# Head norms on Trainium2: the means and the spreads of two neighbouring tiles, issued side by side on the two halves of the array

## The chip, the cores and the metric

The kernel runs on one NeuronCore of one Trainium2 chip. The metric is the time of one execution on the device in microseconds (us); lower is better. Engines are named as in the profile: PE (TensorE, matmul), PEld (its weight loads), DVE (VectorE), ACT (ScalarE), POOL (GpSimd), SP (SyncE, which issues the plain DMAs).

## The reference

Two transformer blocks, run one after the other on 512 tokens of width 1024, all in fp32. What matters here are the norms over a head, of which there are four kinds: queries and keys of the first block (16 heads of 64), queries and keys of the second block (8 heads of 64 each), and the two outputs of the second block's mixer (8 heads of 64, and 4 heads of 128).

```python
def first_block(...):
    h = rms_norm(x, norm1_g)
    q, k, v, bg, cg, xc = split(h @ w_in)
    q = rms_norm(q.reshape(b, nc, CHUNK, 16, 64), q_norm_g)
    k = rms_norm(k.reshape(b, nc, CHUNK, 16, 64), k_norm_g)
    ...                                   # attention, short convolution, gates, w_out, MLP

def second_block(...):
    h = rms_norm_2(x, g_norm1) * (1 + scale1) + shift1
    q_sb = rms_norm_2(to_heads(q_sb, 8), g_q_sb)
    k_sb = rms_norm_2(to_heads(k_sb, 8), g_k_sb)
    y_sb = rms_norm_2(stick_breaking(q_sb, k_sb, v_sb), g_out_sb)          # 8 heads of 64
    y_ml = rms_norm_2(mlstm(q_ml, k_ml, v_ml), g_out_ml) * sigmoid(o_ml)   # 4 heads of 128
    x = x + gate1 * (concat(y_sb, y_ml) @ w_out)
    x = x + gate2 * peer(h2, ...)         # 8 heads x 16 experts for each token, gathered from a table
```

## The kernel before

The 512 tokens go through in two halves of 256 (`hf` 0 and 1). Within a half the work is a fixed list of weight blocks (`SEQ`): each is 1 MB, 1024 rows by 256 columns, loaded by SP into a ring of four, and gives two output tiles `t` of 128 features by 256 tokens. A tile is eight fp32 matmuls, and each fp32 matmul stands in the records as two passes, so a tile is 16 passes and a block 32. A block's name says what it computes: Q1, K1, V1 (4 blocks each), CG, XC, BG, GC, CP, GA, AP, WO (4 each), UP and DN (16 each) for the first block; QKM (4), Q2, K2, V2, VM, OM (2 or 4), WO2 (4), PQ (8) for the second. The order of each engine's work is written out by hand (`half`), with semaphores between the engines.

**Head norms.** Activations lie with features on partitions, so one tile of 128 features holds two heads of 64, and the mean over a head is a sum over partitions. It is done by matmuls. For each of the eight tiles of a kind (`which` 0 to 3: Q1, K1, Q2 with K2, the mixer's output) ACT squares the tile into `scr` (L989, and L1202 for `which` 3), four buffers in turn. `head_mean` (L548 to 561) multiplies the squares by a narrow 128x64 matrix (`half_sel`, or `ml_sel` for heads of 128) that puts the tile's means into its own row of 64 rows of PSUM bank 5: tiles 0 to 3 accumulate in partitions 0 to 63, tiles 4 to 7 in partitions 64 to 127. ACT takes the square root (L1002), DVE the reciprocal (L1410, `hroot`). `head_spread` (L563 to 579) then spreads each row back over the 128 partitions of its tile by a matmul of 64 rows (`spread`, or one column of `ident`), and DVE multiplies the tile by it (`head_scale`, L1415), which counts `hn_done`. For `which` 0 to 2 two spreads share bank 4, side by side in its columns; for `which` 3 spread `i` goes to bank `i % 4`, and spreads 4 to 7 wait until the tile before in the same bank has been scaled.

**Where they stand on PE.** A mean is issued one tile late, so that ACT has had time to square: one after each tile of Q1 and K1 (L769 to 776), and of Q2 and K2. The spreads come two at a time, behind four of K1's and of V1's tiles, behind two of V2's, and around the 16 matmuls of the gates (`w_if`, L833), which accumulate in banks 6 and 7. For `which` 3 all eight means and then all eight spreads stand alone, between the mLSTM and WO2; ACT's squares 4 to 7 wait there for the means of the tiles whose buffer they take.

**Experts.** In half 1, and after it, the experts of half 0 are worked off: POOL gathers rows of 8 KB for 128 tokens (1 MB per slot) and DVE makes a dot product (L1310) and a scaled sum (L1337) of each. `tick` ties them to the weight blocks: behind most blocks of half 1 come two slots. What is left, some 310 of 512 slots, follows after half 1. In half 0 DVE instead sums up 24 modulation blocks (L1485, L1488) behind Q1, K1, V1, CG and XC.

Of the kernel before, what the change touches and what calls it, by code (L numbers as in the profile page):

```python
# [160 lines left out]
def build(nc, a, out):  # L161
    ctx = ExitStack()
    with ctx:
# [322 lines left out]
        def _(pe):  # L486
# [62 lines left out]
            def head_mean(hf, which, i):  # L549

                m = 32 * hf + 8 * which + i
                pe.wait_ge(sq_done, m + 1)
                if which == 3 and i >= 4:
                    sel = ml_sel[:, 3 - i % 4:67 - i % 4]
                else:
                    sel = half_sel[:, 6 - 2 * (i % 4):70 - 2 * (i % 4)]
                o = 64 * (i // 4)
                if i == 0 and which:
                    pe.wait_ge(rt_done, 4 * hf + which)
                pe.matmul(PS[o:o + 64, 5, 0:T], sel, scr[:, m % 4, :], start=i % 4 == 0, stop=i % 4 == 3, **LAX)\  # L560
                    .then_inc(ms_done, 1)

            def head_spread(hf, which, i):  # L563

                m = 32 * hf + 8 * which + i
                if i == 0:
                    pe.wait_ge(rr_done, 4 * hf + which + 1)
                b, c0 = (i % 4, 0) if which == 3 else (4, T * (i % 2))
                if which == 3 and i >= 4:
                    pe.wait_ge(hn_done, m - 3)  # L570
                if which < 3 and i >= 2 and i % 2 == 0:
                    pe.wait_ge(hn_done, m)
                o = 64 * (i // 4)
                if which == 3 and i >= 4:
                    sel = ident[o:o + 64, o + i % 4:o + i % 4 + 1].broadcast_to([64, P])
                else:
                    sel = spread[o:o + 64, 2 * (i % 4):2 * (i % 4) + 2, :].rearrange("p a b -> p (a b)")
                pe.matmul(PS[:, b, c0:c0 + T], sel, hroot[o:o + 64, :], start=True, stop=True, **LAX)\
                    .then_inc(hb_done, 1)
# [182 lines left out]
            def half(hf):  # L762
                for i in range(4):
                    for t in weights_block(NO[hf, Q1, i], h, fresh=4 * hf * KT if i == 0 else None):
                        if hf and 2 * i + t == 1:
                            pe.wait_ge(tok_copy, 10)
                        if 2 * i + t:
                            head_mean(hf, 0, 2 * i + t - 1)
                for which, kind in ((0, K1), (1, V1)):  # L769
                    for i in range(4):  # L770
                        for t in weights_block(NO[hf, kind, i], h, token_major=kind == V1):
                            j = 2 * i + t
                            if j == 0:
                                head_mean(hf, which, 7)
                            elif kind == K1:
                                head_mean(hf, 1, j - 1)
                            if 3 <= j < 7:
                                head_spread(hf, which, 2 * j - 6)
                                head_spread(hf, which, 2 * j - 5)
# [38 lines left out]
                for kind in (Q2, K2, V2):  # L818
                    for i in range(2):
                        for _ in weights_block(NO[hf, kind, i], h, token_major=kind == V2):  # L820
                            if 1 <= m <= 8:
                                head_mean(hf, 2, m - 1)
                            if m >= 10:
                                head_spread(hf, 2, 2 * m - 20)
                                head_spread(hf, 2, 2 * m - 19)
# [3 lines left out]
                head_spread(hf, 2, 4)  # L829
                head_spread(hf, 2, 5)  # L830
# [6 lines left out]
                head_spread(hf, 2, 6)  # L837
                head_spread(hf, 2, 7)
# [18 lines left out]
                for i in range(8):  # L857
                    head_mean(hf, 3, i)
                for i in range(8):
                    head_spread(hf, 3, i)  # L860
# [56 lines left out]
        def _(act):  # L917
# [165 lines left out]
            def half(hf):  # L1083
# [115 lines left out]
                for m in range(8):  # L1199
# [678 lines left out]
```

## Time and profile before

| what | value |
| --- | --- |
| device time, median of 3 runs | 2828.42 us |
| lowest and highest | 2819.37 and 2833.95 us |
| span of the profiled execution, first to last instruction | 2824.7 us |
| PE, DVE, ACT, POOL busy | 2248.1, 1806.8, 667.3, 766.6 us |
| mean granted clock of PE | 0.898 of full speed |
| half 0, first Q1 matmul to the first one of half 1 | 15.67 to 925.02 us |
| half 1, up to its last block's end | 925.02 to about 1992 us |
| experts that are left | about 1992 to 2824.7 us |

The page of the profile gives the span of the profiled execution and no device time of its own; the median of the runs is 3.7 us above that span. In a view of instructions in order of time the columns are the start, how long the group took, the engine, the line of the kernel, the operation with its tiles and shapes, how many were merged, and in brackets how long the engine had been idle before it and what ended that. Matmul records overlap, because a pass's end is drawn after the next one's start: what a matmul costs is read from start to start.

### The profile page before, as it was taken

The numbers are of one execution on the slowest core, as the hardware profiler recorded it, in microseconds if no ns is written. First come the engines' busy times: TensorE is split into PE (matmuls) and PEld (weight loads), VectorE is DVE, ScalarE is ACT, GpSimd is POOL, SyncE is SP. The second block draws the span as 40 slices with busy tenths as digits, with TensorE's granted clock in tenths as the row PEclk, the third lists the DMA queues.
The fourth block names the chain that finished last, engine by engine and source line by source line (L and its number), as shares of the span: only waits on it lengthen the run. The fifth ranks groups of instructions, "written<-read, shape, count | busy, mean of one in ns | idle before, by whom it ended". The sixth has DMA issues, their size and how long they took to land. (4 is left out here: it accounts for less than half of the span.)

```text
span 2824.7 us, 26350 instructions
## 1 busy us (share of the span) xinstructions
PE 2248.1 (80%) x9060; PEld 1659.6 (59%) x9060; DVE 1806.8 (64%) x3668; ACT 667.3 (24%) x1473; POOL 766.6 (27%) x544
## 2 busy tenths in 40 slices
PE   8999999999879998879999998978554555445554
PEld 6787788887668777657788776766211112111211
DVE  4663210012348678777777676759888888888886
ACT  2103212002612311553221126522211111111110
POOL 0000000000000244234433232212373555546551
PEclk9999999999889999999999998989787777777777
DMA  6774334433235699778999884546799999999996
GB/s 239 265 275 138 127 118 155 157 129 139 65 115 209 250 341 398 251 275 320 377 420 413 335 320 151 194 164 228 284 421 421 415 421 422 421 396 422 422 421 269
DMA packets 114661, 798.26 MB, mean 283 GB/s; under 512 B 13280, under 2 KB 16480, under 8 KB 19040
## 3 DMA queue, kind: packets, MB, share of 16 engines
q0 software_dynamic: 74880, 541.10, 47.2%
q1 hardware_dynamic: 39648, 255.47, 24.4%
q8 instruction: 73, 1.20, 0.2%
q14 instruction: 60, 0.49, 0.1%
HBM read 790.23 MB, written 6.29 MB: 282 GB/s over the span
## 5 line engine op out<-in xcount | busy, mean ns | idle before, releaser
L523 PE MATMUL PS<-reg,ring 128*128 128x256 f32 x6016 | 1361.7, 385 | 39.2 <-DVE reg L1405 10.6
L523 PEld LDWEIGHTS PS<-reg,ring 128*128 128x128 f32 x6016 | 1146.1, 193 | 227.0 <-issue 49.0
L473 POOL DMA_INDIRECT uv<-in_expert_uv,experts x322 | 502.3, 1560 | 1872.6 <-DVE experts L1292 879.4
L501 PE MATMUL PS<-uv,spare 128*128 128x512 f32 x276 | 188.4, 832 | 246.4 <-ACT spare L927 246.4
L1337 DVE SCALAR_TENSOR_TENSOR acc<-uv,coef,acc 128x1024 f32<-128x1024 f32 x249 | 319.9, 1285 | 9.0 <-DVE coef L1322 0.2
L1310 DVE CUSTOM_DVE_ANT_0 uv<-uv,h_tok 128x1024 f32<-128x1024 f32 x226 | 269.1, 1219 | 45.6 <-DMA uv<-in_expert_uv,experts 45.4
L501 PEld LDWEIGHTS PS<-uv,spare 128*128 128x128 f32 x276 | 69.8, 269 | 362.8 <-issue 362.8
L501 PE MATMUL PS<-reg,spare 128*128 128x512 f32 x228 | 154.0, 827 | 107.4 <-ACT spare L927 107.4
L934 ACT ACTIVATE acts<-dots 128x2 f32<-128x2 f32 (+1 forms) x192 | 39.1, 204 | 822.6 <-DVE dots L1310 778.1
L501 PEld LDWEIGHTS PS<-reg,spare 128*128 128x128 f32 x228 | 57.8, 267 | 203.0 <-issue 203.0
L473 POOL DMA_INDIRECT reg<-in_expert_uv,experts x114 | 147.8, 1297 | 77.2 <-PE PS L501 49.5
L1310 DVE CUSTOM_DVE_ANT_0 uv<-uv,reg 128x1024 f32<-128x1024 f32 x96 | 116.5, 1223 | 60.2 <-DMA uv<-in_expert_uv,experts 60.1
L1589 DVE TENSOR_TENSOR reg<-PS,reg 128x256 f32<-128x256 f32 x16 | 6.4, 420 | 219.2 <-PE PS L523 219.2
L501 PE MATMUL PS<-ring,spare 128*128 128x512 f32 x152 | 87.7, 716 | 59.6 <-ACT spare L927 59.6
L520 PE MATMUL PS<-ring,reg 128*128 128x256 f32 x512 | 119.3, 389 | 0.0
L473 POOL DMA_INDIRECT ring<-in_expert_uv,experts x76 | 107.1, 1409 | 38.4 <-issue 20.4
L1310 DVE CUSTOM_DVE_ANT_0 reg<-reg 128x1024 f32<-128x1024 f32 x96 | 112.8, 1221 | 3.8 <-DMA reg<-in_expert_uv,experts 3.8
L520 PEld LDWEIGHTS PS<-ring,reg 128*128 128x128 f32 x512 | 97.1, 194 | 19.0 <-issue 6.4
L934 ACT ACT_TABLE_LOAD x59 | 75.7, 1283 | 85.4 <-DVE dots L1310 46.6
L501 PEld LDWEIGHTS PS<-ring,spare 128*128 128x128 f32 x152 | 31.2, 219 | 109.2 <-issue 109.2
L1488 DVE SCALAR_TENSOR_TENSOR uv<-ring,silu_c,uv 128x256 f32<-128x256 f32 x168 | 81.4, 485 | 6.0
L1428 DVE SCALAR_TENSOR_TENSOR reg<-PS,toep 128x128 f32<-128x128 f32 (+1 forms) x64 | 30.9, 483 | 84.2 <-PE PS L603 84.2
(243 smaller groups left out, 2298.7 us busy)
## 6 DMA issues: line engine op xcount, KB each, us to landing
ring<-in_weights SPq DMA_DIRECT2D x228, 1024.0 KB, 5.4
uv<-in_expert_uv,experts POOLq DMA_INDIRECT x322, 12.9
reg<-in_x_t SPq DMA_DIRECT2D x2, 1024.0 KB, 6.2
kv_half<-reg SPq DMA_DIRECT2D x1, 2048.0 KB, 11.4
reg<-in_sub_t SPq DMA_DIRECT2D x2, 1024.0 KB, 4.7
toep<-in_rel_pad SPq DMA_DIRECT2D x16, 128.0 KB, 4.1
x_tokens<-reg SPq DMA_DIRECT2D x2, 1024.0 KB, 9.4
reg<-kv_half SPq DMA_DIRECT2D x1, 2048.0 KB, 16.2
```

The lines of the kernel that those rows point to most:

```text
L473: gp.indirect_dma_start(UV[r], None, a["expert_uv_2"], bass.IndirectOffsetOnAxis(ap=experts[:, e % 256:e % 256 + 1], axis=0))\
L501: mm = pe.matmul(PS[:, 6 + j, :], diag[:, n % 4, :], UV[BUF[s]][:, D + 512 * j:D + 512 * j + 512], start=begins, stop=ends, **LAX)
L520: mm = pe.matmul(out_tile(n, t), mv[:, t * P:(t + 1) * P], w, start=first and k == 0, stop=last and k == KT - 1)
L523: mm = pe.matmul(out_tile(n, t), w[:, t * P:(t + 1) * P], mv, start=first and k == 0, stop=last and k == KT - 1)
L934: act.activation(acts[:, s0 % 16:s0 % 16 + s1 - s0], dots[:, s0 % 16:s0 % 16 + s1 - s0], ACT.Gelu)\
L1310: dve.tensor_tensor_reduce(out=u, in0=u, in1=H2[s // 256][:, s // NSLOT % 2, :], scale=1.0, scalar=0.0, op0=ALU.mult, op1=ALU.add, accum_o ...
L1337: dve.scalar_tensor_tensor(acc[:, :], v, c, acc[:, :], ALU.mult, ALU.add).then_inc(acc_done, 1)
L1428: dve.scalar_tensor_tensor(PROB[:, i % 4, 0:w], PS[:, i % 3, 0:w], HD1 ** -0.5, toep[:, hd % 2, w - 1::-1], ALU.mult, ALU.add).then_inc(s_ ...
L1488: dve.scalar_tensor_tensor(ac, ring[:, n % NRING, k, :], silu_c[:, k:k + 1], ac, ALU.mult, ALU.add)\
L1589: dve.tensor_tensor(x[:, k, :], out_tile(n, t), x[:, k, :], ALU.add).then_inc(evac_sem(n, t), 1)
```

## The change

`head_means` issues the means of an even and an odd tile one right behind the other: the even tile's go to partitions 0 to 63 of bank 5 (columns 0 to 63 of the array), the odd tile's to partitions 64 to 127 (columns 64 to 127). It stands behind every second tile. `head_spreads` issues the spreads of such a pair in the same way: the even tile's row comes from rows 0 to 63 of the array, the odd one's from rows 64 to 127, and they write different banks (4 and 6; for `which` 3 `j` and `4 + j`, so none waits for a scaled tile). The gates' matmuls move from banks 6 and 7 to bank 7 alone. For `which` 3 the pairs are tile `j` of the stick-breaking output with tile `j` of the mLSTM output, and ACT writes its eight squares to eight buffers (`scr` and `spare`), so that none waits for a mean. The number of matmuls, squares and scales stays the same.

```diff
+        def spread_at(which, j, odd):
+            if which == 3:
+                return 4 * odd + j, 0
+            return 4 + 2 * odd, 0
+        def mixed_square(j, odd):
+            return (spare if odd else scr)[:, j, :]
...
-            def head_mean(hf, which, i):
...
+            def head_means(hf, which, j):
+                at = 32 * hf + 8 * which + 2 * j
+                if j == 0 and which:
+                    pe.wait_ge(rt_done, 4 * hf + which)
+                pe.wait_ge(sq_done, at + 2)
+                for odd in range(2):
+                    if which == 3 and odd:
+                        sel = ml_sel[:, 3 - j:67 - j]
+                    else:
+                        sel = half_sel[:, 6 - 2 * j:70 - 2 * j]
+                    src = mixed_square(j, odd) if which == 3 else scr[:, 2 * (j % 2) + odd, :]
+                    pe.matmul(PS[64 * odd:64 * odd + 64, 5, 0:T], sel, src, start=j == 0, stop=j == 3, **LAX)\
+                        .then_inc(ms_done, 1)
...
-            def head_spread(hf, which, i):
...
+            def head_spreads(hf, which, j):
+                if j == 0:
+                    pe.wait_ge(rr_done, 4 * hf + which + 1)
+                if which < 3 and j:
+                    pe.wait_ge(hn_done, 32 * hf + 8 * which + 2 * j)
+                for odd in range(2):
+                    o, (b, c0) = 64 * odd, spread_at(which, j, odd)
+                    if which == 3 and odd:
+                        sel = ident[o:o + 64, o + j:o + j + 1].broadcast_to([64, P])
+                    else:
+                        sel = spread[o:o + 64, 2 * j:2 * j + 2, :].rearrange("p a b -> p (a b)")
+                    pe.matmul(PS[:, b, c0:c0 + T], sel, hroot[o:o + 64, :], start=True, stop=True, **LAX)\
+                        .then_inc(hb_done, 1)
...
-                        if 2 * i + t:
-                            head_mean(hf, 0, 2 * i + t - 1)
+                        if i and t == 0:
+                            head_means(hf, 0, i - 1)
...
-                                head_mean(hf, which, 7)
-                            elif kind == K1:
-                                head_mean(hf, 1, j - 1)
+                                head_means(hf, which, 3)
+                            elif kind == K1 and t == 0:
+                                head_means(hf, 1, i - 1)
                             if 3 <= j < 7:
-                                head_spread(hf, which, 2 * j - 6)
-                                head_spread(hf, which, 2 * j - 5)
+                                head_spreads(hf, which, j - 3)
...
-                            if 1 <= m <= 8:
-                                head_mean(hf, 2, m - 1)
+                            if m in (2, 4, 6, 8):
+                                head_means(hf, 2, m // 2 - 1)
...
-                        mm = pe.matmul(PS[32 * g:32 * g + NML, 6 + g, 0:T], w_if[:, k, g * NML:(g + 1) * NML], H[:, k, :],
+                        mm = pe.matmul(PS[32 * g:32 * g + NML, 7, 0:T], w_if[:, k, g * NML:(g + 1) * NML], H[:, k, :],
...
-                for m in range(8):
-                    if m >= 4:
-                        act.wait_ge(ms_done, 32 * hf + 24 + m - 3)
-                    act.activation(scr[:, m % 4, :], mixed(m), ACT.Square).then_inc(sq_done, 1)
+                for j in range(4):
+                    for odd in range(2):
+                        act.activation(mixed_square(j, odd), mixed(j + 4 * odd), ACT.Square).then_inc(sq_done, 1)
...
-                for m in range(8):
-                    head_scale(hf, 3, m, mixed(m), col("g_out_sb", m))
-                    if m >= 4:
-                        dve.wait_ge(hn_done, 32 * hf + 25 + m)
-                        dve.tensor_tensor(mixed(m), mixed(m), OMT[:, m - 4, :], ALU.mult).then_inc(mixed_gain, 1)
+                for j in range(4):
+                    head_scale(hf, 3, j, 0, mixed(j), col("g_out_sb", j))
+                    head_scale(hf, 3, j, 1, mixed(j + 4), col("g_out_ml", j))
+                    dve.wait_ge(hn_done, 32 * hf + 26 + 2 * j)
+                    dve.tensor_tensor(mixed(j + 4), mixed(j + 4), OMT[:, j, :], ALU.mult).then_inc(mixed_gain, 1)
```

How the instructions stand on PE is shown at three places, before and after apart; the changed kernel's lines are numbered some nine higher, and `x8` of L523 (after: L532) is one tile. First PE in half 0, the last tiles of K1 and the first of V1 (L520, after L529), with K1's means (L560, after L570) and Q1's spreads (L578, after L585). Before:

```order
L523 MATMUL PS<-reg,ring 128x256 x8
L560 MATMUL PS<-scr,half_sel 64x256
L578 MATMUL PS<-hroot,spread 128x256 x2
L523 MATMUL PS<-reg,ring 128x256 x8
L560 MATMUL PS<-scr,half_sel 64x256
L578 MATMUL PS<-hroot,spread 128x256 x2
L523 MATMUL PS<-reg,ring 128x256 x8
L560 MATMUL PS<-scr,half_sel 64x256
L520 MATMUL PS<-ring,reg 128x256 x8
L560 MATMUL PS<-scr,half_sel 64x256
```

Now:

```order
L532 MATMUL PS<-reg,ring 128x256 x8
L585 MATMUL PS<-hroot,spread 128x256 x2
L532 MATMUL PS<-reg,ring 128x256 x8
L570 MATMUL PS<-scr,half_sel 64x256 x2
L585 MATMUL PS<-hroot,spread 128x256 x2
L532 MATMUL PS<-reg,ring 128x256 x8
L529 MATMUL PS<-ring,reg 128x256 x8
L570 MATMUL PS<-scr,half_sel 64x256 x2
```

Every second mean has moved behind the next tile, beside its neighbour; the spreads stand where they stood.

Second PE in half 0 from V2's last tile to the stick-breaking's first logits (L670, after L677), with the gates' matmuls (L833, after L837). Before:

```order
L520 MATMUL PS<-ring,reg 128x256 x8
L578 MATMUL PS<-hroot,spread 128x256 x4
L833 MATMUL PS<-reg,w_if 4x256 x16
L578 MATMUL PS<-hroot,spread 128x256 x2
L670 MATMUL PS<-reg 128x256
```

Now:

```order
L529 MATMUL PS<-ring,reg 128x256 x8
L585 MATMUL PS<-hroot,spread 128x256 x4
L837 MATMUL PS<-reg,w_if 4x256 x16
L585 MATMUL PS<-hroot,spread 128x256 x2
L677 MATMUL PS<-reg 128x256
```

Nothing has moved here; only rows of the array and banks differ.

Third ACT in half 0, the squares of the mixer's output (L1202, after L1204) and the square root behind them (L1002, after L1005). Before:

```order
L1202 ACTIVATE scr<-reg 128x256 x8
L1002 ACTIVATE hroot<-PS,epsc 128x256
```

Now:

```order
L1204 ACTIVATE scr<-reg 128x256
L1204 ACTIVATE spare<-reg 128x256
L1204 ACTIVATE scr<-reg 128x256
L1204 ACTIVATE spare<-reg 128x256
L1204 ACTIVATE scr<-reg 128x256
L1204 ACTIVATE spare<-reg 128x256
L1204 ACTIVATE scr<-reg 128x256
L1204 ACTIVATE spare<-reg 128x256
L1005 ACTIVATE hroot<-PS,epsc 128x256
```

The squares alternate between the two kinds of output and between two tensors.

## Rows read from the trace of the kernel before

**Rows 1.** The page's part on busy time, by engine: us, share, instructions.

```profile
PE 2248.1 (80%) x9060; PEld 1659.6 (59%) x9060; DVE 1806.8 (64%) x3668; ACT 667.3 (24%) x1473; POOL 766.6 (27%) x544
```

**Rows 2.** Stretches: length; PE, PEld, DVE, ACT, POOL busy; clock, DMA share, GB/s.

```profile
957.00:996.00 39.00, 39.00 (x165) 28.11 (x163) 24.66 (x38) 9.47 (x25) 15.22 (x9) 1.00 0.85 331
...
1659.00:1684.00 25.00, 25.00 (x108) 18.84 (x109) 13.26 (x19) 5.69 (x16) 9.79 (x6) 1.00 0.94 362
...
1992.00:2824.00 832.00, 418.84 (x680) 159.29 (x679) 703.92 (x1251) 133.26 (x336) 419.35 (x318) 0.76 0.97 401
```

**Rows 3.** PE in order of time: Q1 of half 0, and a stream without norms.

```profile
23.32 3.72 PE L523 MATMUL PS<-reg,ring 128*128 128x256 f32 x16
26.97 0.65 PE L560 MATMUL PS<-scr,half_sel 128*64 128x256 f32 x2
27.55 3.72 PE L523 MATMUL PS<-reg,ring 128*128 128x256 f32 x16
...
189.72 22.61 PE L523 MATMUL PS<-reg,ring 128*128 128x256 f32 x104
```

**Rows 4.** PE in order of time, K1 of half 0.

```profile
65.01 0.65 PE L560 MATMUL PS<-scr,half_sel 128*64 128x256 f32 x2
65.59 1.13 PE L578 MATMUL PS<-hroot,spread 64*128 64x256 f32 x4
66.64 3.72 PE L523 MATMUL PS<-reg,ring 128*128 128x256 f32 x16
```

**Rows 5.** PE in order of time: the gates, and the mixer norm's means, half 0.

```profile
705.38 3.62 PE L833 MATMUL PS<-reg,w_if 128*4 128x256 f32 x32
...
797.08 0.63 PE L560 MATMUL PS<-scr,half_sel 128*64 128x256 f32 x1
797.14 0.64 PE L560 MATMUL PS<-scr,ml_sel 128*64 128x256 f32 x1
797.51 0.63 PE L560 MATMUL PS<-scr,half_sel 128*64 128x256 f32 x1
```

**Rows 6.** PE in order of time: attention scores of two heads, half 1.

```profile
1135.81 0.70 PE L606 MATMUL PS<-reg 64*128 64x256 f32 x4
1136.35 0.59 PE L603 MATMUL PS<-reg 64*128 64x256 f32 x4
```

**Rows 7.** ACT in order of time, the mixer's norm of half 0.

```profile
794.41 1.33 ACT L1202 ACTIVATE scr<-reg 128x256 f32<-128x256 f32 x4 [1.22 <-DVE reg L1763]
...
799.79 0.47 ACT L1002 ACTIVATE hroot<-PS,epsc 128x256 f32<-128x256 f32 x1 [0.77 <-PE PS L560]
```

**Rows 8.** DVE in order of time, the mixer's norm of half 0.

```profile
803.07 0.48 DVE L1415 SCALAR_TENSOR_TENSOR reg<-reg,par,PS 128x256 f32<-128x256 f32 x1 [1.02 <-PE PS L578]
...
805.63 0.87 DVE L1415 SCALAR_TENSOR_TENSOR reg<-reg,par,PS 128x256 f32<-128x256 f32 x2 [0.37 <-PE PS L578]
...
806.87 0.47 DVE L1415 SCALAR_TENSOR_TENSOR reg<-reg,par,PS 128x256 f32<-128x256 f32 x1
807.38 0.42 DVE L1769 TENSOR_TENSOR reg<-reg 128x256 f32<-128x256 f32 x1
807.72 0.47 DVE L1415 SCALAR_TENSOR_TENSOR reg<-reg,par,PS 128x256 f32<-128x256 f32 x1
...
809.08 0.42 DVE L1769 TENSOR_TENSOR reg<-reg 128x256 f32<-128x256 f32 x1
```

**Rows 9.** PE in order of time, V1 and Q2 of half 1.

```profile
1012.59 1.13 PE L578 MATMUL PS<-hroot,spread 64*128 64x256 f32 x4 [1.73 <-DVE hroot L1410]
1013.65 5.41 PE L520 MATMUL PS<-ring,reg 128*128 128x256 f32 x16
...
1648.78 0.99 PE L560 MATMUL PS<-scr,half_sel 128*64 128x256 f32 x2 [5.11 <-ACT scr L989]
1649.71 5.01 PE L523 MATMUL PS<-reg,ring 128*128 128x256 f32 x16
```

**Rows 10.** Waits of DVE in half 1: who for whom, us, times, longest.

```profile
DVE reg L1523 <- DMA x_tokens<-reg: 11.9, 1, 11.9
```

More of the change, by code:

```diff
@@ L547, in rms @@
                         .then_inc(rms_mm, 1)
-            def head_mean(hf, which, i):
[L551 to L558, printed above, removed]
-                    pe.wait_ge(rt_done, 4 * hf + which)
-                pe.matmul(PS[o:o + 64, 5, 0:T], sel, scr[:, m % 4, :], start=i % 4 == 0, stop=i % 4 == 3, **LAX)\
-                    .then_inc(ms_done, 1)
@@ L764, in half @@
                     for t in weights_block(NO[hf, Q1, i], h, fresh=4 * hf * KT if i == 0 else None):
[L765 removed]
+                        if hf and 2 * i + t == 2:
                             pe.wait_ge(tok_copy, 10)
[L767 to L768 removed]
+                        if i and t == 0:
+                            head_means(hf, 0, i - 1)
                 for which, kind in ((0, K1), (1, V1)):
@@ L856, in half @@
                 mlstm(hf)
[L857 to L860, printed above, removed]
+                for j in range(4):
+                    head_means(hf, 3, j)
+                for j in range(4):
+                    head_spreads(hf, 3, j)
                 pe.wait_ge(hn_done, 32 * hf + 32)
@@ L1198, in half @@
                 act.wait_ge(ml_y, NML * (hf + 1))
-                for m in range(8):
-                    if m >= 4:
-                        act.wait_ge(ms_done, 32 * hf + 24 + m - 3)
-                    act.activation(scr[:, m % 4, :], mixed(m), ACT.Square).then_inc(sq_done, 1)
+                for j in range(4):
+                    for odd in range(2):
+                        act.activation(mixed_square(j, odd), mixed(j + 4 * odd), ACT.Square).then_inc(sq_done, 1)
                 head_root(hf, 3)
@@ L1410, in head_inverse, with head_scale @@
                 dve.reciprocal(hroot[:, :], hroot[:, :]).then_inc(rr_done, 1)
-            def head_scale(hf, which, i, tile, gain):
-                b, c0 = (i % 4, 0) if which == 3 else (4, T * (i % 2))
-                dve.wait_ge(hb_done, 32 * hf + 8 * which + (i if which == 3 else i | 1) + 1)
+            def head_scale(hf, which, j, odd, tile, gain):
+                b, c0 = spread_at(which, j, odd)
+                dve.wait_ge(hb_done, 32 * hf + 8 * which + 2 * j + 1 + (odd if which == 3 else 1))
                 dve.scalar_tensor_tensor(tile, tile, gain, PS[:, b, c0:c0 + T],
@@ L1513, in half @@
                             if 3 <= j < 7:
-                                head_scale(hf, which, 2 * j - 6, tiles[:, 2 * j - 6, :], col(gain))
-                                head_scale(hf, which, 2 * j - 5, tiles[:, 2 * j - 5, :], col(gain))
+                                head_scale(hf, which, j - 3, 0, tiles[:, 2 * j - 6, :], col(gain))
+                                head_scale(hf, which, j - 3, 1, tiles[:, 2 * j - 5, :], col(gain))
                         tick(hf, kind, i)
@@ L1652, in half @@
                     dve.wait_ge(gate_mm, 2 * hf + g + 1)
-                    dve.tensor_scalar(row, PS[32 * g:32 * g + NML, 6 + g, 0:T],
+                    dve.tensor_scalar(row, PS[32 * g:32 * g + NML, 7, 0:T],
                                       par[32 * g:32 * g + NML, COLS["b_i"] + g:COLS["b_i"] + g + 1], None, ALU.add).then_inc(gate_row, 1)
```

26 lines of the change are left out of this document (5 added, 21 removed).

## The prediction

> **What bounds the kernel now.** I read the busy times first: PE is busy for 80% of the span and no other engine for more than 64% [rows 1]. That is an average over stages with different limits, so next come the stretches. In the two where head norms stand inside weight blocks in half 1, PE is busy for the whole of it, at full clock, with DVE at 24.66 of 39 us and 13.26 of 25 us [rows 2]; half 0 looks the same in the view in time. So there every PE microsecond is one of the program. The last 832 us are different: the DMA share is 0.97 at 401 GB/s and PE is busy half of the time [rows 2]. That tail starts when half 1 has ended and always has the same slots left, because `tick` ties expert steps to blocks. I take its length as given, and what the front of the program saves as saved in full, unless the expert steps inside half 1 hold PE up.
>
> **What one mean costs.** Passes of a plain stream follow each other every 0.217 us (22.61 us for 104) or, without the last record's overhang, 0.216 [rows 3]. A tile's 16 passes are 3.45 us. With one mean between two tiles the tiles start 4.23 us apart (23.32 to 27.55) [rows 3]. So a mean costs 0.78 us, of which its two passes are 0.43; the other 0.35 is lost on going from one shape of matmul to another and back. In K1 a mean that is followed by spreads costs 65.59 - 65.01 = 0.58 us, and two spreads, four passes, 66.64 - 65.59 = 1.05 us [rows 4].
>
> **Do two halves of the array run side by side?** For column halves the trace shows it: the gates' 32 passes, which alternate between two column groups, take 3.62 us, where 16 passes of one stream take 3.72 [rows 3, 5]. Means do it too: a pass of `half_sel` starts at 797.08 and one of `ml_sel`, in the other half, at 797.14, while the next of `half_sel` comes only at 797.51 [rows 5]. For row halves the attention scores show it: four passes of the same 64x128 form, two heads on different rows and in different banks, are followed by the next after 0.54 us (1135.81 to 1136.35) [rows 6]. One exposed weight load and two passes fit in that, and four do not. So I take a pair at the price of one: a pair of means costs 0.78, a pair of spreads 1.05 - 2 x 0.216 = 0.62 us. The other bound is no overlap at all, which leaves the spreads at 1.05 and makes a pair of means 0.78 + 0.43 = 1.21.
>
> Here a rule stands against the rows. The Trainium skill, "TensorE: Matmul & The Clock Gate", Part 3, says that matmuls of different tiles start about 4 ns apart but stay in strict program order from start to end. An fp32 matmul is two passes, so by that rule the second tile's first pass would stand behind the first tile's second one, and a pair would cost three passes instead of two, 0.216 us more. The rows disagree: a pass of `ml_sel` runs between two passes of `half_sel` that stand ahead of it in the program [rows 5]. The same skill in "TensorEngine Tiling (Array Packing)", Gotcha 1, says that different row tiles must not write one bank at the same time; the change obeys it with bank 6, and no run shown here tries the opposite.
>
> **The sum.**
> 1. Means alone between tiles. Eight insertions become four in Q1 and in Q2 with K2, and of K1's eight, two that stand alone go (behind tiles 1 and 7). That is 10 per half, 20 x 0.78 = 15.6 us.
> 2. Means ahead of spreads: two per half go, 4 x 0.58 = 2.3 us.
> 3. Spreads of `which` 0 to 2: 12 pairs per half, 24 x 0.43 = 10.3 us. All but one stand in front of PE's own next work, or in the chain PE spread, DVE scale, next spread, which has nothing beside it. One pair in V2 of half 1 stands under an expert step of DVE, so I take 9.8.
> 4. The mixer's norm, half 0. ACT's first four squares are 0.31 us apart (1.33 for four) [rows 7]; the rest waited for means. Now the first pair can start when two squares are there, at about 794.41 + 0.31 + 0.42 + 0.05 = 795.2. PE has been idle, so passes are 0.43 apart [rows 5]: eight of them, the last ending near 795.2 + 7 x 0.43 + 0.63 = 798.8 instead of shortly before 799.79 [rows 7]. That is 0.9. Spreads: DVE starts at 803.07 and ends at 809.50 [rows 8]. Now it goes scale, scale, gain: 0.40 (a pair is 0.87 with 0.47 for one), 0.51, 0.34 apart, 1.25 for each of four [rows 8], against 0.85 for a pair of spreads at half clock, so DVE sets the pace and ends at 803.07 + 3 x 1.25 + 0.40 + 0.51 + 0.42 = 808.15. That is 1.35. By the same working half 1 gives 1.5 (its clock comes back later) and 0.95. Together 4.7 us.
> 5. Q2 in half 1. PE stands for 5.11 us before the first mean, because ACT is behind with its expert steps, and then runs mean and tile at a lower clock: 0.99 and 5.01 us instead of 0.65 and 3.72, 1.6 us more [rows 9]. The first pair now stands behind one more tile, so 3.45 us of work fill the wait; the squares of both tiles are there 0.5 us later than that of one. The gain is about 2.9 us if the clock falls all the same, and 2.9 + 1.6 = 4.5 if it does not. It fell after a wait of only 1.73 us elsewhere (5.41 instead of 3.72) [rows 9], so I take 2.9. The lower bound is nothing.
> 6. At nothing: the gates in one bank (they write different partitions of it, and each column group keeps its passes), later means for ACT's square buffers (a buffer is next needed two tiles on, and each pair stands behind the tile before that), the added bank for the spreads. SP and POOL have no instruction moved past them. The cover of these is one tile, 3.45 us.
>
> Sum: 15.6 + 2.3 + 9.8 + 4.7 + 2.9 = 35.3 us. The span of 2824.7 becomes 2789.4. The median of the runs was 3.7 above that span, so I predict 2793 us.
>
> **Rivals.**
> A. *The experts take half 1's part back.* In Q1 and K1 the DMA share is 0.85 with blocks of some 9 us, and 0.94 in K2 with blocks of 8.45 [rows 2]; blocks get 0.8 to 1.2 us shorter and each still brings its 3 MB, so the share goes to about 1. If gathers or the store of x, for which DVE waits 11.9 us behind V1 [rows 10], are bound by DMA time and not by PE, Q1 to V1 of half 1 give back 6 x 0.78 + 2 x 0.58 + 8 x 0.43 = 9.3 us, and Q2 with K2 some of its 3. Result 2802 to 2805. Against it: DVE has over 10 us of slack in that 39 us stretch, and the store is issued behind a block, so it moves with PE.
> B. *In-order passes*, the rule above as a mechanism of this kernel: 48 pairs lose 0.216 (10.4 us) and eight pairs of means at half clock 0.43 (3.4). Result 2807. The skill's page is the one named above.
> C. *The halves do not overlap in these shapes.* Then a removed insertion saves only its shape changes: 20 x 0.35 + 4 x 0.15 = 7.6 us; spreads give nothing; the mixer's means, partly overlapped today, take about 2 us more per half; item 5 stays. Sum 7.6 - 4 + 2.9 = 6.5, result 2822. For it speaks only that no pair of just these instructions stands in the trace.
> D. *Slower: starved blocks at half clock.* If the faster blocks outrun the gathers, DVE is late, PE waits for a scale or an inverse, and after each wait a tile runs 1.7 us longer (5.41 against 3.72) [rows 9]. To come out 14 us slower it must cost 49 us, some 20 waits of 0.7 us with a slow tile behind each, in the 24 or so tiles of half 1 that have spreads or means. It decides from a DMA share of 1 held over the whole of Q1 to V1; today it is 0.85.
> E. *More than forecast*: the clock holds behind the shorter waits in V1 and Q2 (1.7 + 1.6 us), and the wait in V1 shrinks too. Result 2786 to 2789.
>
> **Chances.** Forecast 0.62, A 0.14, B 0.06, C 0.10, D 0.03, E 0.05. A measurement of this kernel can tell about 0.5% (14 us) from no change; runs of the kernel before lie 7 us around their median. Faster by more than that hold the forecast, A, B and E: 0.87. Within it lies C: 0.10. Slower is D: 0.03. The range reaches down to E less 6 us of scatter, 2780, and up over A and B to 2810; C and D stay outside.
>
> **What would show it.** Q1 tiles in pairs: two tiles about 7.7 us apart from start to start where they took 8.45, in both halves. The two means' passes start within 10 ns of each other, and two spreads in K1 or V1 take 0.6 instead of 1.05 us. First Q1 matmul of half 1 at 925.0 - 16.4 = 908.6 us. The wait before the first mean of Q2 in half 1 under 2.5 us. The square root of the mixer's norm 0.9 us nearer to its first square. Half 1 ends 35 us earlier, and the tail still takes 832 us. I am wrong if pairs take three or four passes (B, C), or if half 0 gains 16 us and half 1 much less than 19 (A).

## The result, and the profile after

The changed kernel takes 2789.95 us (median of 4 runs, 2786.11 to 2794.34), where the kernel before, on the same chip, takes 2830.61 (2819.37 to 2833.95). The ratio is 0.987, 95% interval 0.985 to 0.989. The prediction was 2793 us, with 2780 to 2810 as its range. The profiled execution has a span of 2788.2 us against 2824.7, so the traces differ by 36.5. The device time of the profiled execution itself, 2789.97, lies 1.8 above its span.

The page after, busy times by engine (before: [rows 1]):

```profile
PE 2211.2 (79%) x9060; PEld 1642.6 (59%) x9060; DVE 1807.0 (65%) x3668; ACT 666.1 (24%) x1473; POOL 771.9 (28%) x544
```

PE has the same 9060 instructions and 36.9 us less busy time; DVE, ACT and POOL changed by 0.2, 1.2 and 5.3. PE in order of time after, Q1 of half 0 (before: [rows 3]). Columns here and below: start, length, engine, line, operation with its tiles, count, and in brackets the idle time before it and who ended it.

```profile
29.93 7.17 PE L532 MATMUL PS<-reg,ring 128*128 128x256 f32 x32
37.03 0.65 PE L570 MATMUL PS<-scr,half_sel 128*64 128x256 f32 x4
37.62 7.17 PE L532 MATMUL PS<-reg,ring 128*128 128x256 f32 x32
44.72 0.65 PE L570 MATMUL PS<-scr,half_sel 128*64 128x256 f32 x4
```

Four passes, two means, take the 0.65 us that two passes, one mean, took. Two tiles with their pair stand 7.69 us apart (37.03 to 44.72), where the two tiles with two means took 8.45. A stream without norms needs 6.91, so a pair costs 0.78.

PE after, K1 of half 0 (before: [rows 4]):

```profile
68.61 0.65 PE L570 MATMUL PS<-scr,half_sel 128*64 128x256 f32 x4
69.19 0.70 PE L585 MATMUL PS<-hroot,spread 64*128 64x256 f32 x4
69.83 3.72 PE L532 MATMUL PS<-reg,ring 128*128 128x256 f32 x16
```

A pair of spreads costs 69.83 - 69.19 = 0.64 us instead of 1.05, and a pair of means ahead of them 0.58. In the mixer's norm each record stands alone, so the overlap can be seen (before: [rows 5]):

```profile
781.77 0.66 PE L570 MATMUL PS<-scr,half_sel 128*64 128x256 f32 x1 [4.02 <-ACT spare L1204]
781.78 0.69 PE L570 MATMUL PS<-spare,ml_sel 128*64 128x256 f32 x1
782.22 0.63 PE L570 MATMUL PS<-scr,half_sel 128*64 128x256 f32 x1
782.26 0.63 PE L570 MATMUL PS<-spare,ml_sel 128*64 128x256 f32 x1
...
788.39 0.63 PE L585 MATMUL PS<-hroot,spread 64*128 64x256 f32 x1
788.40 0.63 PE L585 MATMUL PS<-hroot,ident 64*128 64x256 f32 x1
```

The first passes of two neighbouring means start 10 ns apart, their second passes 40 ns apart and some 0.45 us later, at half clock (0.50 granted from 780 to 784 us).

PE after, Q2 of half 1 (before: [rows 9]):

```profile
1624.13 0.65 PE L570 MATMUL PS<-scr,half_sel 128*64 128x256 f32 x4 [2.31 <-ACT scr L992]
1624.71 7.17 PE L532 MATMUL PS<-reg,ring 128*128 128x256 f32 x32
```

The wait of 5.11 us is 2.31, and the two tiles behind it take 7.17 us, as at full clock. Stretches after (length; busy us and count of PE, PEld, DVE, ACT, POOL; clock, DMA share, GB/s): K1 of half 1, K2 with V2's first block, and the tail (before: [rows 2]).

```profile
941.50:975.10 33.60, 33.60 (x161) 25.77 (x160) 23.18 (x37) 9.01 (x23) 13.81 (x8) 1.00 0.96 374
1628.30:1651.30 23.00, 23.00 (x109) 18.55 (x108) 16.93 (x24) 6.02 (x17) 11.60 (x7) 1.00 0.99 401
...
1956.00:2788.00 832.00, 417.53 (x678) 158.54 (x676) 704.12 (x1251) 133.28 (x336) 424.30 (x318) 0.76 0.97 400
```

The same DMA work stands in shorter blocks: the share goes from 0.85 to 0.96 and from 0.94 to 0.99, and PE is still busy throughout. The tail is the same.

**Where the 36.5 us are.** Each block of weights is 32 passes in every kernel here, so the first pass of each block can be counted out in the view in order of time, and the span cut there. These are lengths in us, each from the start of the first block named to the start of the one behind the last. "Before again", "change again" and "change third" are second and third traces of the two kernels. The blocks left out (the last row) take 393.97 or 393.98 in all fourteen traces.

| stretch | before | before again | change | change again | change third |
|---|---|---|---|---|---|
| up to Q1, half 0 | 15.67 | 15.99 | 15.89 | 15.59 | 15.81 |
| first block of Q1 | 7.65 | 10.58 | 9.91 | 6.98 | 6.98 |
| rest of Q1, K1, V1, half 0 | 96.93 | 96.93 | 88.46 | 88.46 | 88.46 |
| CG to UP's first, half 0 | 281.36 | 284.97 | 278.30 | 280.67 | 286.42 |
| rest of UP, DN, QKM's first, half 0 | 230.86 | 230.46 | 230.78 | 230.89 | 230.46 |
| rest of QKM, Q2, K2, half 0 | 53.66 | 53.65 | 50.69 | 50.69 | 50.69 |
| V2, VM's first, half 0 | 52.60 | 54.17 | 51.48 | 51.54 | 52.10 |
| OM's second, WO2, PQ's first, half 0 | 93.06 | 93.10 | 92.74 | 92.76 | 89.95 |
| Q1, K1, half 1 | 70.98 | 70.98 | 63.64 | 63.64 | 63.64 |
| V1, half 1 | 37.01 | 37.01 | 33.53 | 33.53 | 33.52 |
| CG to UP's first, half 1 | 348.25 | 348.24 | 349.76 | 346.54 | 349.72 |
| DN's last, QKM's first, half 1 | 27.41 | 23.70 | 24.95 | 23.98 | 27.36 |
| Q2, K2, half 1 | 39.76 | 39.92 | 32.34 | 32.34 | 32.33 |
| V2, VM's first, half 1 | 77.33 | 77.35 | 75.75 | 76.52 | 76.72 |
| OM's second, WO2, PQ to its fourth, half 1 | 148.01 | 148.02 | 145.60 | 145.50 | 145.56 |
| PQ's last block, half 1, and the tail | 850.19 | 850.54 | 850.40 | 850.10 | 850.42 |
| blocks left out | 393.97 | 393.98 | 393.98 | 393.97 | 393.98 |

Behind the first block of Q1, the stretches with Q or K repeat to 0.16 us or better from trace to trace of one kernel and hold 26.2 us of the gain (8.47, 2.97, 7.34, 7.42). Several others move by 1 to 8 us with nothing changed. Repeating within a kernel is not the same as being set by the code alone: Q2 with K2 of half 1 took 40.91 us in the kernel before with only the mixer's norm changed, where its own code is the same and took 39.76 and 39.92.

### The profile page after: what moved, and what is told of

Same layout as the page of the kernel before. It is cut to its first block and busy times, and to the rows that moved or that the text cites. A ratio compares the mean times of both kernels' runs of the same rounds, so it can differ in the third digit from the quotient of the medians.

```text
span 2788.2 us, 26350 instructions
## 1 busy us (share of the span) xinstructions
PE 2211.2 (79%) x9060; PEld 1642.6 (59%) x9060; DVE 1807.0 (65%) x3668; ACT 666.1 (24%) x1473; POOL 771.9 (28%) x544
## 5 line engine op out<-in xcount | busy, mean ns | idle before, releaser
L532 PE MATMUL PS<-reg,ring 128*128 128x256 f32 x6016 | 1361.9, 386 | 40.4 <-DVE reg L1407 10.5
L532 PEld LDWEIGHTS PS<-reg,ring 128*128 128x128 f32 x6016 | 1151.1, 194 | 223.3 <-issue 42.3
L482 POOL DMA_INDIRECT uv<-in_expert_uv,experts x322 | 510.3, 1585 | 1833.3 <-DVE experts L1294 865.9
L529 PE MATMUL PS<-ring,reg 128*128 128x256 f32 x512 | 117.8, 385 | 0.0
L529 PEld LDWEIGHTS PS<-ring,reg 128*128 128x128 f32 x512 | 96.7, 192 | 17.4 <-issue 4.9
```

The costliest lines, as they stand in the source:

```text
L482: gp.indirect_dma_start(UV[r], None, a["expert_uv_2"], bass.IndirectOffsetOnAxis(ap=experts[:, e % 256:e % 256 + 1], axis=0))\
L529: mm = pe.matmul(out_tile(n, t), mv[:, t * P:(t + 1) * P], w, start=first and k == 0, stop=last and k == KT - 1)
L532: mm = pe.matmul(out_tile(n, t), w[:, t * P:(t + 1) * P], mv, start=first and k == 0, stop=last and k == KT - 1)
```

## The experiments

**The change again, twice, and the kernel before again.** No edit.

> The change once more, unaltered: a second profiled execution, and its time beside the kernels of this call. If the parts that the forecast did not have (the first tile of 9.91 us, the lm projection's first tile of 9.86, the shorter tiles behind the experts) are chance in the clock, some of them will be gone or elsewhere in this trace, while every pair of means still adds 0.78 us to its two tiles and every pair of spreads 0.63. If they belong to the change, they stand where they stood. Time as before, 2786 to 2794.

> The change once more, beside the others of this call: what they are compared with. 2785 to 2794 us; its pairs of means again 0.78, its pairs of spreads 0.63.

> The kernel before once more, for a second profiled execution: its means again one at a time with 7.65 and 8.45 us per two tiles, its spreads 2.12 us in fours. If the parts off the forecast are chance in the clock, OM's last block in the second half (58.12), the first tile (7.65), the tile behind the experts and V1's third block (11.10) move here by 1 to 4 us with nothing changed; if they are the kernel's, they stand.

The change again measured 2791.70 us, ratio 0.988 (0.986 to 0.991); the third time 2794.22, ratio 0.988 (0.986 to 0.990). The kernel before again was one execution, 2831.35. Their traces are columns of the table. The first block of Q1 is luck: 7.65 and 10.58 us before, 9.91, 6.98 and 6.98 after. From the view of stretches, 11 us from 15.60 on, of the change and of the change again, one kernel:

```profile
15.60:26.60 11.00, 10.71 (x36) 9.00 (x37) 10.31 (x26) 1.26 (x4) 0.00 (x0) 0.72 0.00 0
```

```profile
15.60:26.60 11.00, 11.00 (x52) 9.19 (x52) 10.00 (x25) 1.70 (x6) 0.00 (x0) 1.00 0.25 89
```

The granted clock is 0.72 in one and 1.00 in the other, with 36 and 52 passes in it. DN's last block with QKM's first in half 1 is luck as well (27.41 and 23.70 before, 23.98 to 27.36 after). But OM's second block in half 1 stood at 58.12 us in both traces of before, against what was expected of luck, and WO2's first block in half 0 was 9.86 to 9.92 in all three of the change (8.50 and 8.39 before): those hang on the kernel. The Trainium skill, "TensorE: Matmul & The Clock Gate", Part 1, says that the number of slow matmuls at a kernel's start differs between runs of one kernel; the pair of rows above agrees.

**Position alone.** Means of Q1, K1, Q2 and K2 two in a row at the change's places, both on one column half:

```diff
-                        if 2 * i + t:
-                            head_mean(hf, 0, 2 * i + t - 1)
+                        if i and t == 0:
+                            head_mean(hf, 0, 2 * i - 2)
+                            head_mean(hf, 0, 2 * i - 1)
...
-                            if 1 <= m <= 8:
+                            if m in (2, 4, 6, 8):
+                                head_mean(hf, 2, m - 2)
                                 head_mean(hf, 2, m - 1)
```

> The kernel before, with the means of Q1, K1 and Q2/K2 issued two in a row at the places of the change, but both on the same half of the array's columns (the tile's place in hroot is left as it was): the position alone, without the overlap. By the forecast's terms a place costs its change of shape once per pair instead of once per mean (0.35 us, 20 pairs, and 0.15 to 0.35 at the four places ahead of spreads), so 7.6 us, and the second half's Q2 no longer waits for its first square (2.9 to 5.9 us): 10.5 to 13.5 us less than before, 2815 to 2818 where before measures 2828, and a pair of means costs about 1.21 us, not 0.78. If the means of the change were issued in order all along (the rival of no overlap), this kernel would be as fast as the change in its means: 7.17 us of tile and 0.65 of pair in the trace would stay as they are, and it would be about 10 us behind the change for its spreads and 4.7 to 6 for the mixer's norm.

Measured: ratio 0.9964 (0.9948 to 0.9980), 10 us less, interval 6 to 15. PE in order of time, Q1 of half 0:

```profile
37.26 1.08 PE L560 MATMUL PS<-scr,half_sel 128*64 128x256 f32 x4
38.27 7.17 PE L523 MATMUL PS<-reg,ring 128*128 128x256 f32 x32
45.37 1.08 PE L560 MATMUL PS<-scr,half_sel 128*64 128x256 f32 x4
```

Two tiles and their means take 8.11 us: 0.34 less than before, and 0.42 more than the change. The first is one change of shape there and back (the next run tests that), the second is the overlap. Q2 with K2 of half 1 is 33.10 us, 6.66 less than before.

**Shape alone.** The means of half 0 as products of all 128 columns, one by one where they were:

```diff
...
+                if hf == 0:
+                    r = o + 2 * (i % 4)
+                    sel = gate2[:, 200 + 3 - i % 4:328 + 3 - i % 4] if which == 3 and i >= 4 else gate2[:, 70 - r:198 - r]
...
+                if hf == 0:
+                    pe.matmul(PS[:, 5, 0:T], sel, scr[:, m % 4, :], start=i == 0, stop=i == 7, **LAX).then_inc(ms_done, 1)
+                    return
```

> The kernel before, with the means of the first half as products of the full 128 columns (a selector of 128 columns in an unused part of gate2, all eight into the same sums), so that the array's shape is the same as the tiles' around them; issued one by one where they were. If 0.35 us of the 0.78 is the change of shape there and back, a mean costs 0.43 us as a spread does: the Q1 blocks of the first half fall from 8.45 to 7.75 us, 20 x 0.35 + 4 x 0.15 to 0.35 = 7.6 to 8.4 us less than before. If it is something else (the selector's load, the wait for the square), they stay at 8.45 and nothing is gained. The sums of the first half's means are the same numbers.

Measured: ratio 0.9992 (0.9975 to 1.0008). PE in order of time, Q1 of half 0:

```profile
41.73 0.59 PE L570 MATMUL PS<-scr,gate 128*128 128x256 f32 x2
42.16 3.62 PE L529 MATMUL PS<-reg,ring 128*128 128x256 f32 x16
45.61 0.59 PE L570 MATMUL PS<-scr,gate 128*128 128x256 f32 x2
```

A mean is 42.16 - 41.73 = 0.43 us and the two tiles 7.77: the mechanism is as expected. The rest of Q1 with K1 and V1 of half 0 is 4.44 us shorter, Q2 with K2 2.28. But the stretch with the mixer's norm is 3.1 us longer (96.14). Some 1.7 of them are its eight wide means, which no longer overlap:

```profile
791.27 6.54 PE L570 MATMUL PS<-scr,gate 128*128 128x256 f32 x16 [4.08 <-DVE reg L1775]
```

The same sixteen passes in the kernel before, its first and its last row, take from 794.92 to 799.75, 4.8 us:

```profile
794.92 2.37 PE L560 MATMUL PS<-scr,half_sel 128*64 128x256 f32 x5 [3.67 <-DVE reg L1763]
...
798.00 1.75 PE L560 MATMUL PS<-scr,ml_sel 128*64 128x256 f32 x5
```

What the other 1.4 us are, no row here shows. The 3.6 us of gain that are left (4.44 + 2.28 - 3.1) lie within the interval, 2 us less (from 7 less to 2 more), where the expectation had 7.6 to 8.4. It had not costed the overlap of the mixer's means, which the kernel before already had. That a change between these shapes costs 0.34 us is shown by the 0.43. "TensorEngine Tiling (Array Packing)" in the Trainium skill, section "Key Properties", says that changing the tiling mode drains TensorE; it names no price. The rows here give the price of such a change and do not show a drain.

**Spreads alone.** Tiles j and j+4, on the two row halves, into banks 4 and 6; means as before:

```diff
-                b, c0 = (i % 4, 0) if which == 3 else (4, T * (i % 2))
+                b, c0 = (i % 4, 0) if which == 3 else (4 + 2 * (i // 4), 0)
...
-                                head_spread(hf, which, 2 * j - 6)
-                                head_spread(hf, which, 2 * j - 5)
+                                head_spread(hf, which, j - 3)
+                                head_spread(hf, which, j + 1)
...
```

> The kernel before, with the spreads of Q1, K1 and Q2/K2 issued as pairs from the two row halves of hroot into banks of their own (tiles j and j+4, so the means stay as they were). By the forecast 24 pairs save 0.43 us each: 9.8 to 10.3 us less than before, the pair standing at about 0.63 us in the trace instead of 1.06. If spreads did not overlap, or if the second bank were what matters and not the row half, it would be 0 and 10 respectively; the next kernel tells the two apart.

**The change without the overlap of its spreads.** Still two banks, but each pair from one row half:

```diff
-                    o, (b, c0) = 64 * odd, spread_at(which, j, odd)
+                    r = j if which == 3 else same_half(j, odd) // 2
+                    o, (b, c0) = 64 * (odd if which == 3 else same_half(j, odd) % 2), spread_at(which, j, odd)
```

> The change, with its spreads of Q1, K1 and Q2/K2 still two at a time into two banks, but both from the same half of the rows of hroot: the overlap of the spreads alone is taken away. By the forecast it loses 24 x 0.43 us = 10.3 us against the change, about 26 to 30 us less than before; each pair stands at about 1.05 us. If two banks were enough for the gain (a drain of one bank that both had waited for), it would be as fast as the change.

Measured: spreads alone 0.9956 (0.9940 to 0.9972), 12 us less. The change without the overlap of its spreads 0.9907 (0.9888 to 0.9926), 26 us less; the change measured 33 to 37 us less. K1 in order of time, without that overlap:

```profile
68.73 1.13 PE L590 MATMUL PS<-hroot,spread 64*128 64x256 f32 x4
69.79 3.72 PE L536 MATMUL PS<-reg,ring 128*128 128x256 f32 x16
```

1.06 us in two banks but one row half, 0.64 in two banks and two halves: a second bank alone gains nothing, the second row half does. Whether two halves overlap into one bank wasn't tried, so the second bank may be needed with it.

**The second half's wait alone.** Its means of Q2 and K2 one tile later:

```diff
-                            if 1 <= m <= 8:
+                            if hf == 0 and 1 <= m <= 8:
                                 head_mean(hf, 2, m - 1)
+                            if hf and 2 <= m <= 8:
+                                head_mean(hf, 2, m - 2)
+                                if m == 8:
+                                    head_mean(hf, 2, 7)
```

> The kernel before, with the second half's means of Q2 and K2 one tile later, one by one: the wait for the first square alone is moved, nothing is paired. By the forecast's term 2.9 to 5.1 us less than before; the traces so far (place against before, over the two blocks of Q2) say 5.1 to 5.6. If the wait only moved on to the second mean, because the squares come as late as the means, it would be 0, with the 5.11 us of wait seen a tile later.

Measured: ratio 0.9972 (0.9954 to 0.9989), 8 us less, interval 3 to 13. PE in order of time:

```profile
1650.77 0.65 PE L560 MATMUL PS<-scr,half_sel 128*64 128x256 f32 x2 [1.67 <-ACT scr L993]
1651.34 3.72 PE L523 MATMUL PS<-reg,ring 128*128 128x256 f32 x16
```

The wait is 1.67 instead of 5.11 and the clock does not fall. Q2 with K2 takes 33.90 instead of 39.76, and V2's first block 0.44 more for the mean moved into it: 5.4 us.

**The mixer's norm alone, and the change without it.** ACT's squares, their buffers, the banks of the spreads and DVE's scales are as in the change too.

```diff
...
-                for i in range(8):
+                for i in (0, 4, 1, 5, 2, 6, 3, 7):
                     head_mean(hf, 3, i)
-                for i in range(8):
+                for i in (0, 4, 1, 5, 2, 6, 3, 7):
                     head_spread(hf, 3, i)
...
```

> The kernel before, with the mixer's norm alone as in the change: squares, means and spreads in the order of tile j and its neighbour on the other half, squares of the second four in a buffer of their own, eight banks for the spreads, scale in the same order. By the forecast 4.7 us less than before (2.25 in the first half, 2.45 in the second); by the block starts of the change 2.17 and 4.05, 6.2 in all. If the second half's 4 us were chance in the clock, OM's last block would stand at 55.7 to 56.7 us instead of 54.1.

> The change with the mixer's norm put back as it was before (squares, means, spreads and scale of 0 to 7 in turn, four banks). By the forecast's term it is 4.7 us slower than the change beside it. By the traces so far it is 0 to 1.5 us slower: over OM's last block, the four blocks of WO2 and PQ's first the new order gains 0.4 to 0.9 us in the first half, not 2.2, because the tile behind it runs longer, and about as little in the second; the mixer's norm alone measured no gain.

Measured: alone 1.0008 (0.9993 to 1.0023), no gain; the change without it 2791.16 us beside 2794.22 for the change, ratios 0.987 and 0.988 to before, no loss. OM's second block, WO2's first and PQ's first, half 0: 46.80, 8.92 and 9.83 us with the old norm in the changed kernel, 44.88, 9.86 and 10.30 in the change. The norm does gain 1.9 us, and the next blocks give back 1.4. Stretches of PE of the change without it, where WO2 begins at 800.88:

```profile
799.00:803.00 4.00, 2.12 (x5) 1.79 (x6) 1.71 (x5) 0.00 (x0) 0.00 (x0) 0.50 0.27 86
803.00:807.00 4.00, 4.00 (x16) 3.31 (x16) 0.45 (x1) 0.00 (x0) 0.00 (x0) 0.77 1.00 410
```

And of the change, where it begins at 794.23:

```profile
793.00:797.00 4.00, 2.77 (x7) 2.27 (x8) 1.09 (x3) 0.00 (x0) 0.00 (x0) 0.50 0.43 129
797.00:801.00 4.00, 4.00 (x13) 3.27 (x12) 0.16 (x1) 0.00 (x0) 0.00 (x0) 0.62 0.95 395
```

In both the norm leaves PE at half clock (0.50 granted). WO2 starts earlier in the change, but a longer piece of it then runs slow: the clock is up again some 4 us after its start in the one, near 6 in the other. In half 1 the stretch around the norm is 145.71 us with the old norm and 145.50 to 145.60 with the new. The 58.12 us of OM in the kernel before are another matter. In two stretches of it, 16 and 20 us into the block,

```profile
1810.70:1814.70 4.00, 3.23 (x12) 2.44 (x11) 3.33 (x9) 1.00 (x2) 0.00 (x0) 0.76 0.50 209
1814.70:1818.70 4.00, 4.00 (x18) 3.34 (x17) 1.09 (x1) 0.63 (x2) 0.00 (x0) 0.81 0.00 0
```

the clock fell; in the change without the new norm it is 1.00 at the same place:

```profile
1781.20:1785.20 4.00, 3.22 (x16) 2.54 (x16) 3.33 (x9) 0.98 (x3) 0.00 (x0) 1.00 0.51 217
```

So that loss goes without the mixer's norm being touched (145.75 us too with the second half's wait alone). Nor does the new norm keep it away: 12 us into the block the granted clock is 0.62 with position alone, which has the old norm, and 0.61 in the change without the overlap of its spreads, which has the new one.

**Four means at a time.** On four quarters of 32 columns, in two places per kind; spreads in pairs from row quarters:

```diff
...
+                for g in range(4):
...
+                    pe.matmul(PS[32 * g:32 * g + 32, 5, 0:T], sel, src, start=r == 0, stop=r == 1, **LAX)\
...
-                            if m in (2, 4, 6, 8):
-                                head_means(hf, 2, m // 2 - 1)
+                            if m in (4, 8):
+                                head_means(hf, 2, m // 4 - 1)
```

> The change carried on: means four at a time, on four quarters of 32 columns, in two places per kind instead of four, and spreads in pairs from row quarters. If an overlapped mean costs next to nothing beyond the change of shape, a place of four costs what a place of two does (0.78 us, 0.58 ahead of spreads), so half of the places go: in each half five places of 0.78 and one of 0.58, 2 x 4.5 = 9 us less than the change, 2780 to 2782. If four quarters run only two at a time, or if four streams share the rows' read port, a place costs 1.1 to 1.2 us and it comes out within 2 us of the change. Slower than the change by 2 to 5 us if the later means hold up the root and reciprocal, which wait for the last of them, but the last place is where it was.

> The means four at a time once more, beside the change on the same chip: 7 to 10 us faster than it (10 places fewer of 0.78, two fewer of 0.58, less what the clock takes back), against 0 to 2 if the gain seen before was a difference of chips.

Measured: 2785.05 us, ratio 0.985 (0.983 to 0.987), and again 2783.79, ratio 0.985 (0.983 to 0.987), where the change on the same chip took 2794.22. PE in order of time, Q1 of half 0 and Q2 of half 1, of the second:

```profile
48.61 0.64 PE L571 MATMUL PS<-scr,half_sel 128*32 128x256 f32 x8
49.18 7.17 PE L534 MATMUL PS<-reg,ring 128*128 128x256 f32 x32
...
1621.62 0.64 PE L571 MATMUL PS<-scr,half_sel 128*32 128x256 f32 x8 [0.59 <-ACT scr L994]
```

Eight passes, four means, take the 0.64 us of two. Half 0's rest of Q1 to V1 is 85.47 us (88.46 in the change), its rest of QKM with Q2 and K2 49.11 (50.69), and in half 1 60.67 (63.64) and 29.06 (32.33), where the wait is now 0.59 us. V1 of half 1 gives back 1.8 to 2.4 (35.34 and 35.92 for 33.53). That is 10.8 less 1.8 to 2.4, about 8.7; the ratios say 8.5 and the medians 10 (the two intervals overlap slightly, so the size is rough). It beats both kernels.

## Why the prediction was right, and where it was not

**Items 1 and 2, means between tiles and ahead of spreads: right.** In the stretch of the rest of Q1, K1 and V1 in half 0, fifteen means became eight pairs: five places fewer of 0.78 and two of 0.58, 5.1 us, and eight pairs of spreads give 8 x 0.43 = 3.4. That is 8.5 for the 8.47 measured. Position and overlap each hold about half: 0.34 and 0.42 a pair. The first block of Q1 has one mean less to do, and still took 2.3 us more in the first trace, by luck of the clock.

**Item 3, spreads: right.** 0.64 instead of the 0.62 taken, and 12 us (5 either way) by themselves for the forecast's 9.8. V1 of half 1 gained 3.48, where V1 of half 0 gained 1.79 (33.52 to 31.73). The other 1.69 is the tile behind the 1.73 us wait: that wait is still there, but no slow clock follows it in any of the three traces of the change. With the mixer's norm alone changed, V1's code and that wait as before, the slow tile was gone too (35.33 us), so overlapped spreads aren't needed to end it; in the change without their overlap it was there (5.41 us, V1 36.92). What ends it is open.

**Item 4, the mixer's norm: wrong, 4.7 forecast, about 0.6 found.** Beside the change without it, the stretch goes from 93.23 to 92.74 us in half 0 and from 145.71 to 145.60 in half 1. Its own working was near (2.17 us of 2.25 in half 0). The failing step is that what ends earlier was counted as saved in full: behind it WO2 begins at half clock, which holds on 1.4 us longer in its blocks and PQ's. In half 1 the 2.4 us that the stretch lost (148.01 to 145.60) are gone too in kernels that leave its norm as it was (145.57 to 145.75).

**Item 5, the wait of Q2: right in kind, too small.** Forecast 2.9, with 4.5 if the clock stays up. It stays up: behind the wait of 2.31 us two tiles took their usual 7.17, behind the 1.67 one took 3.72. Q2 with K2 lost 7.42 us where half 0, with no such wait, lost 2.97, so item 5 is 4.45, the upper of the two values; alone it gave 5.4. The failing step is the choice that the clock would fall as it did after V1's wait: that one wait was no rule.

**Rival A** is seen, small: CG's second and third block of half 1 take 18.6, 17.8 and 17.9 us in the change and 16.0 and 15.6 before, at a DMA share of 1.02. PE waits there for ACT, which has waited for the store of x, and then runs slow:

```profile
1025.74 1.62 PE L532 MATMUL PS<-reg,ring 128*128 128x256 f32 x3 [3.09 <-ACT reg L1015]
```

```profile
ACT reg L1015 <- DMA x_tokens<-reg: 16.0, 1, 16.0
```

PE waited 1.97 us at this place in the kernel before, and ACT 14.8 for the store. That is 2.3 us back; over the whole stretch to UP it does not show against its scatter (346.5 to 349.8). **Rival B** fell by the mixer's records, **C** by the pairs in Q1 and by position alone, **D** by PE's full busy time at a share of 0.96 and 0.99. **E**, the clock behind the short waits, came true for V1 and Q2 (1.7 + 1.5 us), though V1's wait did not shrink, and item 4 lost as much. So the sum of 35.3 us was met by 36.5, but with parts off by 1.5 to 4 us on both sides, and a single pair of traces moves by several us with nothing changed. The costs of a pair of means and of spreads were right; that the rest cancelled to 1.2 us is luck. The scatter on top is as large: 4 us lie between the medians of the changed kernel in its three measurements, and up to 16 between single runs. The forecast also added 3.7 us to go from span to device time, a median set against the span of another execution. One execution's device time lies 1.8 above its own span, and these 1.9 are most of the 3 us between 2793 and 2789.95.

**The landmarks.** The first Q1 of half 1 stood at 911.50, not 908.6. The first block's clock (2.3 us longer instead of 0.8 shorter) and the mixer's norm (0.3 gained, not 2.25) account for 5.0 the wrong way, and CG to UP was 3.1 shorter by chance. PQ's last block in half 1 began 36.7 us earlier, for 35 forecast, and it takes with the tail 850.40 us for 850.19.

What stays open: why the clock falls in OM of half 1 in both traces of the kernel before, and in none of the change. The stretch's own instructions don't decide it: with the same ones there, it falls in position alone too, and not with the second half's wait alone. That it hangs on when the stretch comes is a guess; no run moved its start alone.

## What to carry to other kernels

A small matmul of another shape between large ones costs here 0.43 us for its passes and 0.34 for the changes of shape, so gather such matmuls in one place first (two of one half already save 0.34), and put them on different column or row groups then (0.42 more, and four cost as much as two). Don't count in full what ends earlier in front of a stretch at half clock (here 1.9 us gained and 1.4 given back): read what the granted clock does in the first tiles behind it. And take a second trace of the same kernel before explaining a difference of 1 to 4 us by a change.

## What the runs showed of the hardware

- Passes of four column quarters run side by side at the price of one: 0.64 us for eight passes, as for two.
- The scatter from trace to trace of one kernel can be put in numbers: 7.65 and 10.58 us before, and 6.98 to 9.91 in the change, for the first block of 32 passes; 89.95 to 92.76 around the mixer's norm; 23.70 and 27.41 for DN's last block with QKM's first; 278.30 to 286.42 from CG to UP. The stretches with Q or K behind the first block repeat to 0.16 us or better, and the blocks left out to 0.01. So those stretches can be compared far more sharply than a kernel's times.
- With one short wait of almost the same length the clock may fall or hold (V1's 1.73 us, 1.74 with the mixer's norm changed: 0.76 granted in the next 4 us in the kernel before, 1.00 with only the mixer's norm changed):

```profile
1012.00:1016.00 4.00, 3.41 (x11) 2.56 (x12) 2.74 (x5) 0.00 (x0) 0.00 (x0) 0.76 1.02 424
```

```profile
1008.20:1012.20 4.00, 3.41 (x15) 2.76 (x16) 2.75 (x5) 0.00 (x0) 0.00 (x0) 1.00 1.01 420
```

The first row is the stretch behind that wait in the kernel before, the second the same place in the kernel with the mixer's norm alone.
